# First block of a two-block transformer: state-space steps placed behind products, the branch product in pieces, silu from Tanh

## The reference, cut to what matters

```python
u = rms_norm(h, mix_norm[l])
(z_s, xbc, dt_s, qkv, z_d, b_d, a_d, gate_s, gate_d) = jnp.split(u @ w_in[l], split_points, axis=-1)
# mamba2_branch, 32 heads of 64 in 4 groups
xbc = silu(causal_depthwise_conv(xbc, conv_w, conv_b))
y = ssd_chunked(xs, dt, a, Bm, Cm) + xs * d_skip
y_s = group_rms_norm(y * silu(z_s)) * norm_w
# deltanet_branch, 8 heads of 128
qkv = silu(causal_depthwise_conv(qkv, conv_w))
q, k = l2_norm(q) * 128 ** -0.5, l2_norm(k)
o = gated_delta_rule_chunked(q, k, v, g, beta)      # inverse of a triangular matrix, then states
y_d = rms_norm(o) * norm_w * silu(z_d)
merged = sigmoid(gate_s) * (y_s @ ssm_w_branch[l]) + sigmoid(gate_d) * (y_d @ dn_w_branch[l])
h = h + merged @ w_out[l]
```

## Time and profile before

| | us |
|---|---|
| median of 3 runs (3724.16 to 3727.95) | 3724.76 |
| the profiled execution | 3724.71 |
| its span, first to last instruction | 3722.9 |

### The profile page before, as it was taken

The page is one execution under the profiler, slowest core; times in us unless marked ns, Lnnn a source line. Parts: engine busy times, 40 slices in busy tenths (PEclk is TensorE's granted clock), DMA queues, the critical chain, the costliest instruction groups (busy, mean ns, idle before and its releaser), DMA issues.

```text
span 3722.9 us, 51208 instructions
## 1 busy us (share of the span) xinstructions
PE 3548.9 (95%) x21932; PEld 3154.1 (85%) x21932; DVE 1744.2 (47%) x3861; ACT 549.7 (15%) x1157; POOL 259.8 (7%) x352
## 2 busy tenths in 40 slices
PE   8999996999999999987899999999999999999998
PEld 8998883879999988864889987787889986878898
DVE  6643116715666633045516633901268429111486
ACT  1112113011101022012101110021121000210211
POOL 0200000300100100001200200010003000100021
PEclk9999996999999999986999999999999999999999
DMA  5444430034445444410045434434435444344344
GB/s 178 170 146 149 149 134 1 1 104 152 168 155 170 170 136 149 159 68 0 9 150 177 163 136 154 151 125 149 136 136 168 150 148 157 124 147 147 114 170 136
DMA packets 70978, 493.97 MB, mean 133 GB/s; under 512 B 7648, under 2 KB 11104, under 8 KB 11616
## 3 DMA queue, kind: packets, MB, share of 16 engines
q1 hardware_dynamic: 70752, 490.70, 38.7%
HBM read 489.62 MB, written 1.05 MB: 132 GB/s over the span
## 4 chain that ended last, share of the span: by engine, by line
PE 88%; DVE 8%; ACT 2%; issue 1%; DMA 0%; SPq 0%; POOL 0%; DVEq 0%; ACTq 0%
PE bank L304 79%; PE bank L1471 1%; PE bank L1483 1%; PE bank L1478 1%; DVE arena L1175 1%; DVE arena L1182 1%; PE bank L1432 1%; PE bank L1425 1%; DVE arena L754 1%; DVE arena L752 1%; DVE arena L756 1%; DVE arena L751 0%; DVE arena L1176 0%; PE bank L1969 0%; PE bank L2000 0%
## 5 line engine op out<-in xcount | busy, mean ns | idle before, releaser
L304 PE MATMUL bank<-xT,ring 128*128 128x256 f32 (+1 forms) x7232 | 1383.3, 352 | 19.9 <-DVE xT L665 10.8
L304 PEld LDWEIGHTS bank<-xT,ring 128*128 128x128 f32 x7232 | 1231.6, 193 | 160.3 <-issue 25.3
L304 PE MATMUL bank<-arena,ring 128*128 128x128 f32 (+1 forms) x5200 | 888.1, 327 | 0.0
L304 PEld LDWEIGHTS bank<-arena,ring 128*128 128x128 f32 x5200 | 801.7, 192 | 70.0 <-issue 3.0
L304 PE MATMUL bank<-arena 128*128 128x128 f32 x5280 | 625.6, 275 | 2.4 <-DVE arena L756 2.3
L304 PEld LDWEIGHTS bank<-arena 128*128 128x128 f32 x5280 | 607.3, 192 | 3.1 <-DVE arena L756 3.1
L1100 DVE SCALAR_TENSOR_TENSOR arena<-arena,par 128x256 f32<-128x256 f32 x288 | 118.1, 480 | 197.8 <-ACT arena L904 197.8
L751 DVE TENSOR_TENSOR arena<-ring 128x512 f32<-128x512 f32 x198 | 136.9, 691 | 131.4 <-PE bank L304 107.8
L1772 DVE SCALAR_TENSOR_TENSOR arena<-arena,par 128x256 f32<-128x256 f32 x480 | 190.7, 479 | 0.0
L849 POOL TENSOR_TENSOR arena<-arena 128x128 f32<-128x128 f32 x66 | 38.9, 590 | 1605.1 <-DVE arena L803 897.1
L1332 POOL TENSOR_TENSOR arena<-arena,cst 128x512 f32<-128x512 f32 x56 | 72.9, 1334 | 1056.5 <-DVE xT L1251 1008.8
(11 more groups left out here) (264 smaller groups left out, 2556.6 us busy)
## 6 DMA issues: line engine op xcount, KB each, us to landing
ring<-w SPq DMA_DIRECT2D x462, 1024.0 KB, 4.8
hT<-hT_d SPq DMA_DIRECT2D x4, 256.0 KB, 3.8
arena<-memT_d SPq DMA_DIRECT2D x1, 1024.0 KB, 7.9
outT<-hT SPq DMA_DIRECT2D x4, 256.0 KB, 2.2
cst<-cst_d SPq DMA_DIRECT2D x1, 924.5 KB, 6.8
arena<-dmask_d SPq DMA_DIRECT2D x1, 768.0 KB, 10.3
par<-p SPq DMA_DIRECT2D x2, 376.5 KB, 6.7
par<-p SPq DMA_DIRECT2D x2, 216.0 KB, 5.0
```

The costliest lines, as they stand in the source:

```text
L304: ins = self.e.matmul(out, lhsT, rhs, start=start, stop=stop)
```

## The change

It moves work within the mixer of both layers of the first block.

- TensorE makes `x_rows` i right behind `xbc` product i+3, `cum` and `cum_t` now stand there too, and `z_s` product 0 stands before `cb`.
- A loop of 19 steps makes one product each (`z_s` 1 to 7, then `qkv` 0 to 11); in the first 16 a state-space step's `y` and `seg` follow the product. `z_d` and the gates follow the loop. The chunks of weights lie in the new order.
- `y_norm` is within the loop: VectorE adds the four squares (two new operations per group) and TensorE makes one matmul for a group and not four. ScalarE copies the sums and takes Ln and Exp once for all four groups.
- Silu of `qkv`, `z_s` and `z_d` becomes Tanh on ScalarE and one more VectorE operation (`gate_z`, `qkv_silu`: (1 + tanh) * x on 128x512). The gate by z becomes a scalar_tensor_tensor with the factor 0.5. VectorE halves the `qkv` taps once per layer. The function set of Exp and Tanh is loaded; there are six more table loads in all.
- `branch_s` is made in 16 halves of 8 matmuls: seven between the `qk_norm` sums and one behind them, one before `kq`, one before the levels, one each behind `wt`, `state`, `v1` and `o`, and two between the `o_norm` sums. VectorE reads its banks at eight places (`branch_s(i)`).

```diff
+    def part(self, key, acts, tiles, half):
+        if half == 0:
+            self.held = self.open_bulk(*key)
+        for k in range(half * tiles // 2, (half + 1) * tiles // 2):
+            ins = self.mm(self.held[:, 0:S], self.tile(), acts[:, k, :], k == 0, k == tiles - 1)
+        if half:
+            ins.then_inc(self.sems.bulk_done, 1)
...
+ROWS_AT, CUM_AT, CUM_T_AT = 3, 5, 7
+STEPS = 19
+BESIDE = [("z_s", i) for i in range(1, 8)] + [("qkv", i) for i in range(12)]
+Z = [("z_s", i) for i in range(8)] + [("z_d", i) for i in range(4)]
...
-        spec += many(L, "xbc", 12, "act") + many(L, "qkv", 12, "act") + many(L, "z_s", 8, "act") + many(L, "z_d", 4, "act")
+        spec += many(L, "xbc", 12, "act") + many(L, "z_s", 8, "dve") + many(L, "qkv", 12, "act") + many(L, "z_d", 4, "dve")
...
+            if p % 4 == 2 and p > 4:
+                spec += [((L, "y_norm", p // 4 - 1), "act")]
...
+    def conv_tanh(i):
+        e.wait_ge(sems.conv_done, upto(L, "conv_done", 12 + i + 1))
+        if i >= 2:
+            e.wait_ge(sems.qkv_ready, upto(L, "qkv_ready", i - 1))
+        e.activation(m.qkv_th[:, i % 2], m.qkv[:, 2 * i:2 * i + 2, :], ACT.Tanh).then_inc(sems.qkv_tanh, 1)
+        seen.up("qkv_tanh")
+    def z_tanh(i):
+        e.wait_ge(sems.bulk_done, BULK.filled(L, *Z[i]))
+        b = bk[BULK.bank(L, *Z[i])]
+        if i >= 2:
+            e.wait_ge(sems.bulk_read_dve, BULK.read(L, *Z[i - 2]))
+        e.activation(m.z_th[:, i % 2], b.rearrange("p (t n) -> p t n", n=S), ACT.Tanh, scale=0.5).then_inc(sems.z_tanh, 1)
+        seen.up("z_tanh")
...
+    z_tanh(0)
+    for p in range(3):
+        decay(p)
+    for p in range(STEPS):
+        name, i = BESIDE[p]
+        if name == "z_s":
+            z_tanh(i)
+        else:
+            conv_in(12 + i)
+            if i:
+                conv_tanh(i - 1)
+        if p + 3 < 16:
+            decay(p + 3)
+        if p % 4 == 0 and p:
+            g = p // 4 - 1
...
+            e.activation(m.sq_s, m.xbc[:, 4 * g:4 * g + 4, :], ACT.Square).then_inc(sems.squares_ready, 1)
+            seen.up("squares_ready")
+        if p % 4 == 2 and p > 4:
+            g = p // 4 - 1
+            e.wait_ge(sems.chain_done, CHAIN.filled(L, "y_norm", g))
+            e.activation(m.rn_s[:, g, :], bk[CHAIN.bank(L, "y_norm", g)][:, 0:S], ACT.Copy).then_inc(sems.chain_read_act, 1)
+    conv_tanh(11)
+    e.preload_act_table_set(LN_EXP)
+    e.wait_ge(sems.chain_read_act, CHAIN.read(L, "y_norm", SSM_GROUPS - 1))
+    e.activation(m.rn_s, m.rn_s, ACT.Ln, scale=1.0 / 512, bias=EPS).then_inc(sems.act_step, 1)
+    e.wait_ge(sems.act_step, seen.up("act_step"))
+    e.activation(m.rn_s, m.rn_s, ACT.Exp, scale=-0.5).then_inc(sems.rnorm_ready, 1)
+    seen.up("rnorm_ready")
+    e.preload_act_table_set(EXP_TANH)
+    for i in range(8, 12):
+        z_tanh(i)
...
+    for n in range(12):
+        conv(n)
+        if ROWS_AT <= n < ROWS_AT + 8:
+            rows(n - ROWS_AT)
+        if n == CUM_AT:
+            running_sums()
...
+        stt(dst, m.z_th[:, i % 2], 1.0, b.rearrange("p (t n) -> p t n", n=S), ALU.add, ALU.mult).then_inc(sems.bulk_read_dve, 1)
...
+        stt(x, m.qkv_th[:, i % 2], 1.0, x, ALU.add, ALU.mult).then_inc(sems.qkv_ready, 1)
...
-        tt(x, x, m.z_s[:, p, :], ALU.mult).then_inc(sems.y_gated, 1)
+        stt(x, x, 0.5, m.z_s[:, p, :], ALU.mult, ALU.mult).then_inc(sems.y_gated, 1)
...
+    for p in range(STEPS):
+        name, i = BESIDE[p]
+        if name == "z_s":
+            gate_z(i)
+        else:
+            conv(12 + i)
+            if i:
+                qkv_silu(i - 1)
         if p + 1 < 16:
             mix(p + 1)
-        y_out(p)
+        if p < 16:
+            y_out(p)
         if p + 3 < 16:
             seg(p + 3)
+        if p % 4 == 1 and p > 4:
+            g = p // 4 - 1
+            e.wait_ge(sems.squares_ready, upto(L, "squares_ready", g + 1))
+            tt(m.sq_s[:, 0:2, :], m.sq_s[:, 0:2, :], m.sq_s[:, 2:4, :], ALU.add).then_inc(sems.dve_step, 1)
+            e.wait_ge(sems.dve_step, seen.up("dve_step"))
+            tt(m.sq_s[:, 0, :], m.sq_s[:, 0, :], m.sq_s[:, 1, :], ALU.add).then_inc(sems.y_summed, 1)
+            seen.up("y_summed")
...
+        if i in (2, 4, 6):
+            branch_s(i // 2 - 1)
...
+    t.product((L, "z_s", 0), xT)
...
+    for p in range(STEPS):
+        t.product((L, *BESIDE[p]), xT)
+        if p < 16:
+            bank = t.open_chain(L, "y", p)
+            e.wait_ge(sems.mix_ready, upto(L, "mix_ready", p + 1))
+            for hh in range(2):
+                f = (2 * p + hh) * SSM_P
+                out = bank[hh * SSM_P:(hh + 1) * SSM_P, :]
+                e.matmul(out[:, 0:S], m.xdt[:, 0, f:f + SSM_P], m.seg[:, p % 3, hh, 0:S], start=True, stop=False)
+                ins = e.matmul(out[:, P:S], m.xdt[:, 1, f:f + SSM_P], m.seg[:, p % 3, hh, S:384], start=False, stop=True)
+            ins.then_inc(sems.chain_done, 1)
         if p + 3 < 16:
             spread("seg", p + 3, 0)
-        for k in range(4):
-            ins = e.matmul(bank[:, 0:S], const("ones"), m.sq_s[:, k, :], start=(k == 0), stop=(k == 3))
+        if p % 4 == 2 and p > 4:
+            g = p // 4 - 1
+            bank = t.open_chain(L, "y_norm", g)
...
+            e.wait_ge(sems.y_summed, upto(L, "y_summed", g + 1))
+            e.matmul(bank[:, 0:S], const("ones"), m.sq_s[:, 0, :], start=True, stop=True).then_inc(sems.chain_done, 1)
+    for name in ("z_d", "gate_s", "gate_d"):
+        for i in range(4):
+            t.product((L, name, i), xT)
+    halves = iter(range(16))
+    def beside():
+        i, half = divmod(next(halves), 2)
+        t.part((L, "branch_s", i), m.xbc, 2 * KD, half)
...
+    e.wait_ge(sems.normed, upto(L, "normed", SSM_GROUPS))
     for i in range(8):
+        if i:
+            beside()
         norm_sums("qk_norm", i, SSM_GROUPS)
...
+    beside()
     e.wait_ge(sems.normed, upto(L, "normed", SSM_GROUPS + 8))
     for i in range(8):
         bank = t.open_chain(L, "kv_rows", i)
...
     heads("wt", lambda hd, out: e.matmul(out, m.k_sc[:, hd, 1, :], inv_t[:, 2 * hd + 1, :], start=True, stop=True))
+    beside()
     e.wait_ge(sems.chain_read_act, CHAIN.read(L, "u0", 1))
     heads("state", lambda hd, out: e.matmul(out, m.k_sc[:, hd, 0, :], m.v_new[:, hd, 0, :], start=True, stop=True))
+    beside()
     e.wait_ge(sems.chain_read_act, CHAIN.read(L, "state", 1))
     heads("v1", v1)
+    beside()
...
         norm_sums("o_norm", i, SSM_GROUPS + 8)
-    e.wait_ge(sems.normed, upto(L, "normed", SSM_GROUPS))
-    for i in range(8):
-        t.features((L, "branch_s", i), m.xbc, 2 * KD)
```

More of the change, by code:

```diff
@@ L917, in first_act @@
             conv_silu(n - 1)
[L918 to L928, removed]
+    conv_silu(11)
+    e.preload_act_table_set(EXP_TANH)
     e.wait_ge(sems.chain_read_dve, CHAIN.read(L, "cum", 0))
@@ new lines, in first_dve @@
+    for n in range(12):
+        conv(n)
[3 more added lines that the diff above has]
+            running_sums()
+        if n == CUM_T_AT:
+            e.wait_ge(sems.chain_done, CHAIN.filled(L, "cum_t", 0))
+            b = bk[CHAIN.bank(L, "cum_t", 0)]
+            e.tensor_copy(m.acT[0:3 * SPREAD, :], b[0:3 * SPREAD, 0:S]).then_inc(sems.chain_read_dve, 1)
+    e.wait_ge(sems.small_by_act, upto(L, "small_by_act", 5))
+    e.tensor_copy(m.ksc[:, :, 0], m.suf).then_inc(sems.dve_step, 1)
@@ L1160, in first_dve @@
+    gate_z(0)
     for g in range(SSM_GROUPS):
@@ L1391, in first_pe @@
         ins.then_inc(sems.chain_done, 1)
+    for i in range(1, 12):
+        t.product((L, "xbc", i), xT)
+        if ROWS_AT <= i < ROWS_AT + 8:
+            rows(i - ROWS_AT)
+        if i == CUM_AT:
+            bank = t.open_chain(L, "cum", 0)
+            e.wait_ge(sems.dt_ready, upto(L, "dt_ready", 1))
+            la = m.loga
+            e.matmul(bank[:, 0:NSM], const("upto"), la[:, 0, :], start=True, stop=True)
+            e.matmul(bank[:, NSM:NSM + SSM_HEADS], const("upto"), la[:, 1, 0:SSM_HEADS], start=True, stop=False)
+            e.matmul(bank[:, NSM:NSM + SSM_HEADS], const("ones"), la[:, 0, 0:SSM_HEADS], start=False, stop=True)
+            e.matmul(bank[:, NSM + SSM_HEADS:2 * NSM], const("upto"), la[:, 1, SSM_HEADS:NSM], start=True, stop=True)
+            e.matmul(bank[:, 2 * NSM:2 * NSM + 8], const("after"), la[:, 0, ACOL:NSM], start=True, stop=True).then_inc(sems.chain_done, 1)
+        if i == CUM_T_AT:
+            bank = t.open_chain(L, "cum_t", 0)
+            e.wait_ge(sems.split_ready, upto(L, "split_ready", 1))
+            for tt_ in range(NT):
+                ins = e.transpose(bank[0:3 * SPREAD, tt_ * P:(tt_ + 1) * P], m.split[:, tt_].rearrange("p i n -> p (i n)"), ident)
+            ins.then_inc(sems.chain_done, 1)
+    t.product((L, "z_s", 0), xT)
+    e.wait_ge(sems.features_ready, upto(L, "features_ready", 12))
     for g in range(SSM_GROUPS):
@@ L1513, in first_pe @@
         ins.then_inc(sems.chain_done, 1)
+    beside()
     for i in range(4):
```

(6 more changed lines are left out.)

211 lines of the change are left out of this document (106 added, 105 removed).

## The result

| | us |
|---|---|
| before, median of 4 runs | 3724.46 (3719.65 to 3727.95) |
| after, median of 4 runs | 3564.91 (3564.68 to 3567.65) |
| ratio | 0.9572, 95% interval 0.9559 to 0.9585 |
| profiled span after | 3563.0 |
| predicted | 3565, range 3550 to 3594 |

The first lines of the page after, to be read beside the earlier trace rows: busy time of each engine with its share of the span, and TensorE's clock in 40 slices.

A forecast was written before the change was run, and what follows sets the result against it. TensorE was busy 95% of the span, so only its waits and low-clock stretches could give time. Terms summed to 206.4 us per layer against 283.4 and 289.1, gaining 159.7 from 3724.7: 3565 us, range 3550 to 3594.

The forecast's parts named there:

- (1): Between products: the 32 `x_rows` transposes take 3.6 us per layer, `cb` and three `seg` together 3.3.
- (2): Sixteen state-space steps behind products: `y` and `seg` take 15.8 us per layer; `y_norm`, down to 4 matmuls, 1.7.
- (3): Loop: a ring (copy waits for Exp, Exp for VectorE's `seg`) turns in 8.5 us against 7.94; waits sum to 2.8.
- (4): Behind the last gate product: TensorE waits 2.75 us per layer, plus 1.0 because the clock may fall.
- (5): `qk_norm`: eight sums and eight halves of `branch_s` take 34.6 us per layer, and TensorE does not wait.
- (6): From `kv_rows` to the levels: 24.2 us per layer, with two halves (6.9) fitting into TensorE's idle time.
- (7): Levels to first `o_norm` sum: 99.0 us; four halves add 13.8, covered waits save 2.7, a faster first level 1.5.
- (8): Tail, `o_norm` sums to `branch_d`: 15.6 us with waits of 2.1 and 3.1, plus 2.0 for low clock, 17.6.
- Rival A: Loop: the ring's turns have nothing in hand, so (3) is 9.8 us and the time 3579; chance 10%.
- Rival B: The halves of `branch_s` hide nothing and are paid in full, 55 us per layer; time 3629; chance 4%.
- Rival C: TensorE's clock stays at the low level in the mixed loop and `qk_norm`; time 3931, slower; chance 3%.
- Rival D: `z_s` or the sums come on TensorE's path, a bank being free later; time 3724 within 7; chance 1%.

The follow-up runs named there:

- e1: Changed kernel without the 16 halves: `branch_s` made in eight whole chunks behind `o_norm`, as before the change; 3623.18 us.
- e6: e5 with ScalarE's Exp of `seg` p+2, not p+3, behind the copy and tap of product p; 3546.22 us.
- e3: Changed kernel with two extra VectorE products of 128x512, results unused, behind the convolution in each of a layer's twelve `qkv` steps; 3585.74 us.
- e2: Kernel before the change with only the 16 halves of `branch_s` put in, products and state-space steps in the old order; 3668.96 us.
- e5: Changed kernel with halves behind `wt`, `state`, `v1` moved ahead of the first `qk_norm` sum and behind the third and fourth `o_norm` sum; 3546.39 us.

## Why the prediction was right, point by point

The sum came out at 206.4 us per layer and the time at 3565, measured 3564.91. Part of this closeness is luck. Several terms were off by 0.5 to 2 us per layer, in both directions.

- **(1), (2) Steps behind products: right, slightly too cheap.** A step is 8.04 us, 0.1 over the 7.94 of the sum. The 0.1 stands 16 times in a layer, 1.6 us. Nearly all of it is between a product and the `y` behind it: 7.00 us from start to start (345.95 to 352.95), where 16 such matmuls take 6.91. The sum had the changes between products and small matmuls at nothing, and the high end of the range had 45 of them at 0.15. In e1 the whole first part gains 98.8 us alone, and the loop shows no wait for the cycle of the earlier trace rows but the two of (3).
- **(3) The ring: right as a mechanism, mis-sized.** Predicted were a turn of 8.5 us and 2.8 us of waits at `y` 12 to 14; measured were a turn of 8.22, and 0.63 and 0.41 us ahead of `y_norm` in steps 10 and 14 only. No `y` waited. The waits stood at another link than the predicted one, VectorE's sum of the squares, which runs late when the ring is late: in e6, with the ring open, they are gone. VectorE's timeline of the changed kernel shows where the 0.3 went:

```profile
420.31 2.46 DVE L1164 SCALAR_TENSOR_TENSOR arena<-arena,par 128x256 f32<-128x256 f32 x6 [3.07 <-ACT arena L936]
422.69 0.68 DVE L1237 SCALAR_TENSOR_TENSOR arena<-arena 128x512 f32<-128x512 f32 x1
423.29 0.95 DVE L1263 TENSOR_TENSOR arena<-arena 128x768 f32<-128x768 f32 x1
```

  The 128x512 operation (L1237) was taken at 0.75, the duration of one that stood alone. In a stream what counts is the distance to the next start, 0.60 (422.69 to 423.29). With the other links the same way, convolution 2.38, `mix` 0.87, `y_out` 0.85, `seg` to Exp 1.42 and Exp to copy 0.75, behind 1.35 ahead of the convolution, a turn is 8.22. Rival A, with 9.8 us for this term, is false. But e3 shows how near it was: with 1.2 us more per turn, `y` waits as well, the waits cost 7.16 us per layer and the clock another 2.7.
- **(4) Behind the last gate product: right, and the clock too cheap.** The wait was 2.72 for the predicted 2.75. Behind it the first sum with its half took 6.07 us (575.72 to 581.79) where the others take 4.31: 1.76 for the clock, and not 1.0. ScalarE's table load there took the 1.28 us of the earlier trace rows, with the square right behind it.
- **(5) `qk_norm`: right.** 4.31 us per sum and half, no wait. Rival B is false, for the reason given against it, and in e2 the halves alone gain 53 us.
- **(6) `kv_rows` to levels: right.** 23.87 us (611.97 to 635.84) for 24.2, with the two halves inside it.
- **(7) Levels to `o_norm`: right in sum, by two errors that cancel.** 99.07 us (635.84 to 734.91) for 99.0. From the start of the levels to `u0` are 70.9 us (635.84 to 706.70), 0.8 less than before and not 1.5: the first level did not become fast, its first group still takes 5.60 us at a granted clock of 0.70. From `u0` to the sum the waits gave back 3.4 us and not 2.7.
- **(8) The tail: right, and the clock too dear.** 15.57 us (734.91 to 750.48) for 15.6. The rows show waits of 1.96 and 2.86 behind the drain of the last sum, which with the drain are the 2.1 and 3.1 of the sum. From the start of `branch_d` to the read of its first bank were 8.58 us. A product with its drain lasts 7.07 at the high level, so the clock took 1.5 and not 2.0.
- **The errors together.** Per layer: the step +1.6, (3) -1.8, (4) +0.8, (6) -0.3, (7) +0.1, (8) -0.5. They cancel to -0.1, which is luck.
- **Rival C is false.** Loop and `qk_norm` were granted 1.00 and 0.98. The sentence of the Trainium skill ("TensorE: Matmul & The Clock Gate", A second HAM failure mode: psum-queue depth-cycling) warned of short idles between groups with banks in rotation. This loop does rotate its banks and changes between three kinds of matmul each 8 us, and had no fall in 134 us; its only idles were 0.63 and 0.41 us. With longer ones, in e3, the clock did fall.
- **Rival D is false:** neither `z_s` nor the sums waited for a bank.
- **What the prediction missed.** It counted 2.75, 2.1 and 3.1 us of waits per layer, with 3 us for the clock behind them, as fixed parts of the sum. They were not: e5 removes them by moving three halves, for 18.5 us.

## What to carry to other kernels

To hide one engine's chain behind another's bulk work, compare two numbers with the step: the busy sum of each engine, and the length of any ring through the in-order queues. The second one decided here (free with one order, 20 us with the other), and it is taken from start to start of instructions in a stream, not from the durations of lone ones. Work that can be cut into pieces belongs first where the bulk engine waits and its clock falls behind the wait; a fixed wait in a sum is a place to fill.

## What the runs showed of the hardware that was not expected

- **Two short waits close together were followed by the low level, another such pair was not.** In e3 waits of 1.74 and 2.01 us, with 1.2 us of small matmuls between them, were followed by a product of 9.26 us. In the same layer waits of 2.38 and 1.03 us were followed by one of 7.07. Layer 1 has the same waits, with products of 9.31 and 7.07. The page of the profile, with clock 9 in each slice, hides all of this. The stretch itself (e3, in the columns of the earlier trace rows) does not:

```profile
426.00:436.00 10.00, 6.25 (x23) 4.57 (x23) 8.86 (x20) 2.58 (x5) 0.00 (x0) 0.69 0.18 51
```

- **Changing between large and small matmuls cost nothing in most places, and 0.09 us in one.** In the changed kernel a product before transposes takes 6.91 us (268.06 to 274.97) and a half before a sum 3.45 (582.65 to 586.10), as without a change. Only between a product and `y` are 7.00 us; why is open. VectorE and ScalarE work on other banks meanwhile, with 126 GB/s of DMA, and the clock stays at its high level of 2.4 GHz.
- **The same matmuls behind the same waits run at either level.** The `y_norm` groups took 1.97 us in layer 0 of the kernel before and up to 3.75 in layer 1, in one execution, and in e2 the layers had changed places. Here a term of a sum that stands behind waits of 2 us has two prices, 6 us apart over the four groups, and nothing in the rows ahead of it says which one it gets.
